# A hybrid block pair on one core: the recurrence's root from tanh(-x) and exp(2x), and gate tiles ahead of the first transposes in two attention layers

## The reference, cut to what matters

```
r = sigmoid(x W_a + b_a);  i = sigmoid(x W_x + b_x)
log_a = -8 * r * softplus(-lam)
a = exp(log_a);  u = sqrt(-expm1(2 * log_a)) * (i * x)
h[t] = a[t] * h[t-1] + u[t];   y = h * silu(x W_g)
```

```
S = scale * Q K^T + bias or mask;  P = softmax(S);  O = P V
y = (O * silu(h W_z)) W_out
```

## Time and profile before

| what | value |
|---|---|
| median of 3 runs | 2391.98 us |
| lowest, highest | 2387.72, 2394.45 us |
| the profiled execution | 2391.33 us |
| its span | 2389.6 us |
| mean granted TensorE clock | 0.944 |
| TensorE matmuls busy | 2102.4 us (88%) |
| VectorE busy | 1273.9 us (53%) |
| ScalarE busy | 889.1 us (37%) |
| GpSimd busy | 524.6 us (22%) |

### The profile page before, as it was taken

One profiled execution on the slowest core, in us unless ns is written; L12 is line 12 of the kernel. 1 busy time (PEld: TensorE's weight loads), 2 busy tenths in 40 slices (PEclk: granted clock), 3 DMA queues, 4 the chain that ended last, 5 costly groups with the idle time before them and its releaser, 6 DMA issues.

```text
span 2389.6 us, 25010 instructions
## 1 busy us (share of the span) xinstructions
PE 2102.4 (88%) x10118; PEld 1611.7 (67%) x10118; DVE 1273.9 (53%) x1756; ACT 889.1 (37%) x1281; POOL 524.6 (22%) x422
## 2 busy tenths in 40 slices
PE   5899998999988998999798886979879988878986
PEld 3687765788556887678597763767657755555865
DVE  6886664727389233544525446164455466544273
ACT  4225455311274223322322343256433344533232
POOL 3852121405146401232210101102021001102001
PEclk9999999999987998999899998989989999989998
DMA  2242110234221533535256421711212201122211
GB/s 110 87 156 78 36 54 18 91 108 152 90 88 53 159 106 106 176 115 163 92 146 172 98 79 44 160 36 53 71 58 87 90 18 36 36 71 97 88 71 53
DMA packets 53138, 215.26 MB, mean 90 GB/s; under 512 B 6048, under 2 KB 23104, under 8 KB 32672
## 3 DMA queue, kind: packets, MB, share of 16 engines
q1 hardware_dynamic: 22896, 162.54, 19.5%
q0 software_dynamic: 9488, 35.94, 5.4%
q10 hardware_dynamic: 20640, 15.19, 3.0%
HBM read 196.14 MB, written 17.50 MB: 89 GB/s over the span
## 4 chain that ended last, share of the span: by engine, by line
PE 59%; DVE 14%; ACT 4%; issue 3%; DMA 2%; ACTq 1%; POOL 1%; DVEq 0%; PEldq 0%
PE bank L477 16%; PE bank L478 16%; PE bank L479 16%; PE bank L476 2%; ACT ring_high L434 2%; DVE ring_low L439 2%; DVE root L1513 2%; DMA ring<-slabs 2%; DVE root L1204 1%; PE bank L1140 1%; PE bank L2761 1%; DVE sq L1208 1%; PE bank L2787 1%; ACTq L2085 1%; DVE lru_x L1526 1%
## 5 line engine op out<-in xcount | busy, mean ns | idle before, releaser
L439 DVE TENSOR_TENSOR ring_low<-ring,ring_high 128x2048 fp32r<-128x2048 f32 x136 | 329.8, 2426 | 473.2 <-ACT ring_high L434 473.2
L477 PE MATMUL bank<-h_high,ring_high 128*128 128x512 f32 x1248 | 512.7, 411 | 70.7 <-DVE ring_low L439 37.4
L434 ACT ACTIVATE ring_high<-ring 128x2048 fp32r<-128x2048 f32 x145 | 277.5, 1914 | 627.7 <-PE bank L479 582.5
L478 PE MATMUL bank<-h_low,ring_high 128*128 128x512 f32 x1248 | 497.4, 399 | 0.0
L479 PE MATMUL bank<-h_high,ring_low 128*128 128x512 f32 x1248 | 495.7, 397 | 0.0
L477 PEld LDWEIGHTS bank<-h_high,ring_high 128*128 128x128 f32 x1248 | 241.3, 193 | 155.1 <-issue 68.4
L478 PEld LDWEIGHTS bank<-h_low,ring_high 128*128 128x128 f32 x1248 | 242.3, 194 | 51.0 <-issue 3.5
L479 PEld LDWEIGHTS bank<-h_high,ring_low 128*128 128x128 f32 x1248 | 241.2, 193 | 52.5
L477 PE MATMUL bank<-gated_high,ring_high 128*128 128x512 f32 x256 | 106.1, 415 | 27.2 <-issue 20.8
L439 POOL TENSOR_TENSOR ring_low<-ring,ring_high 128x2048 fp32r<-128x2048 f32 x9 | 43.0, 4783 | 335.0 <-ACT ring_high L434 335.0
L478 PE MATMUL bank<-gated_low,ring_high 128*128 128x512 f32 x256 | 104.2, 407 | 0.0
(11 more groups left out here) (500 smaller groups left out, 4035.1 us busy)
## 6 DMA issues: line engine op xcount, KB each, us to landing
ring<-slabs SPq DMA_DIRECT2D x149, 1024.0 KB, 4.8
s_outputs<-s_ca POOLq DMA_DIRECT2D x4, 1152.0 KB, 8.1
x<-xT SPq DMA_DIRECT2D x2, 2048.0 KB, 9.1
s_b<-s_br POOLq DMA_DIRECT2D x8, 512.0 KB, 4.1
s_rows<-s_powers POOLq DMA_DIRECT2D x16, 256.0 KB, 6.9
s_inputs<-s_w POOLq DMA_DIRECT2D x8, 512.0 KB, 3.5
s_ck<-s_outputs POOLq DMA_DIRECT2D x1, 4096.0 KB, 23.5
s_wv<-s_inputs ACTq DMA_DIRECT2D x8, 512.0 KB, 6.0
```

The costliest lines, as they stand in the source:

```text
L434: act.activation(self.ring_high[:, self.splits_before[s] % AHEAD, :], self.ring[:, s % RING, :], ACT.Copy)\
L439: dve.tensor_tensor(self.ring_low[:, s % RING, :], self.ring[:, s % RING, :], self.ring_high[:, self.splits_before[s] % AHEAD, :].bitcast( ...
L477: pe.matmul(out, w[0], x[0], start=start, stop=False)
L478: pe.matmul(out, w[0], x[1], start=False, stop=False)
```

## The change

It does three things. In the recurrence q comes as (exp(2x) + 1) * tanh(-x), with the new exponential on ScalarE and one instruction on VectorE instead of three; ScalarE now writes q, so it waits for the scan of four tiles earlier. In the sliding-window stage z_0 and z_1 are computed after scores(1) and the loop computes z_(j+2) up to j = 5. In the latent stage z_0 comes after scores(1), and the loop computes z_(h/2+1) with scores(h+2), up to h = 12. Banks, weight order, evacuations and splits follow.

```diff
@@ more_sections
-    for j in range(9):
-        if j < 8:
-            cols = np.r_[256 * j + span(0, 64), 256 * j + 128 + span(0, 64)]
-            add("mla_kz", [("c_w_ukv", span(k * P), cols) for k in range(2)])
-        if j > 0:
-            add("mla_kz", tile("c_w_in", KD, span(1056 + (j - 1) * P)))
+    for j in range(8):
+        cols = np.r_[256 * j + span(0, 64), 256 * j + 128 + span(0, 64)]
+        add("mla_kz", [("c_w_ukv", span(k * P), cols) for k in range(2)])
+        add("mla_kz", tile("c_w_in", KD, span(1056 + j * P)))
@@ stage_lru, ratios (VectorE)
                     dve.wait_ge(th.sem, th.at(m))
-                    ln(dve, dve.tensor_scalar(q, t, 1.0, None, ALU.add))
-                    ln(dve, dve.reciprocal(q, q))
-                    dve.scalar_tensor_tensor(out=q, in0=t, scalar=2.0, in1=q, op0=ALU.mult, op1=ALU.mult)\
+                    dve.scalar_tensor_tensor(out=q, in0=q, scalar=1.0, in1=t, op0=ALU.add, op1=ALU.mult)\
                         .then_inc(rt.sem, 1)
@@ stage_lru, decays (ScalarE)
                     if m >= BUFS:
-                        act.wait_ge(rt.sem, rt.at(m - BUFS))
-                    C.achain.link(act, act.activation(t, L.R[:, m, :], ACT.Tanh, scale=-1.0))
+                        act.wait_ge(scanned.sem, scanned.at(m - BUFS))
+                    act.activation(t, L.R[:, m, :], ACT.Tanh, scale=-1.0)
+                    C.achain.link(act, act.activation(q, L.R[:, m, :], ACT.Exp, scale=2.0))
                     act.activation(L.R[:, m, :], L.R[:, m, :], ACT.Exp).then_inc(th.sem, 1)
@@ stage_swa, TensorE
             scores(0)
             scores(1)
+            for j in range(2):
+                C.gemm(pe, zb[j], C.H.tiles(KD), seen)
...
                 if j + 2 < NJ:
                     scores(j + 2)
-                C.gemm(pe, zb[j], C.H.tiles(KD), seen)
+                    C.gemm(pe, zb[j + 2], C.H.tiles(KD), seen)
@@ stage_swa, ScalarE
-            exps(0)
-            exps(1)
+            def evac_z(j):
+                C.split_high(act, zb[j][0])
+                C.full(act, zb[j][0])
+                act.activation(L.Z[:, j, :], C.bank[zb[j][0].b][:], ACT.Copy).then_inc(C.bank_read[zb[j][0].b], 1)
+
+            for j in range(2):
+                evac_z(j)
+                exps(j)
...
                     exps(j + 2)
+                    evac_z(j + 2)
@@ stage_mla, TensorE
             scores(0)
             scores(1)
+            C.gemm(pe, zb[0], C.H.tiles(KD), seen)
             C.read(pe, L.v_uses[-1])
...
                 if h + 2 < H:
                     scores(h + 2)
-                if h % 2 == 0:
-                    C.gemm(pe, zb[h // 2], C.H.tiles(KD), seen)
+                    if h % 2 == 0:
+                        C.gemm(pe, zb[h // 2 + 1], C.H.tiles(KD), seen)
@@ stage_mla, ScalarE (evac_z as above)
             keys(0)
             exps(0)
+            evac_z(0)
             exps(1)
...
                     exps(h + 2)
+                    if h % 2 == 0:
+                        evac_z(h // 2 + 1)
```

More of the change, by code:

```diff
@@ L1536, in decays @@
                 for m in range(b, b + NB):
-                    t = C.sq[:, m % BUFS, :]
+                    t, q = C.sq[:, m % BUFS, :], C.root[:, m % BUFS, :]
                     act.wait_ge(scaled.sem, scaled.at(m))
                     if m >= BUFS:
-                        act.wait_ge(rt.sem, rt.at(m - BUFS))
-                    C.achain.link(act, act.activation(t, L.R[:, m, :], ACT.Tanh, scale=-1.0))
+                        act.wait_ge(scanned.sem, scanned.at(m - BUFS))
+                    act.activation(t, L.R[:, m, :], ACT.Tanh, scale=-1.0)
+                    C.achain.link(act, act.activation(q, L.R[:, m, :], ACT.Exp, scale=2.0))
                     act.activation(L.R[:, m, :], L.R[:, m, :], ACT.Exp).then_inc(th.sem, 1)
@@ L2545, in stage_swa @@
     NJ = 8
-    sb, pb, ob, zb = [[C.take_bank() for _ in range(TC)] for _ in range(2)], [], [], []
+    sb, pb, ob, zb = [[C.take_bank() for _ in range(TC)] for _ in range(2)], [], [], [C.take_tile(KD) for _ in range(2)]
     for j in range(NJ):
@@ L2550, in stage_swa @@
             sb.append([C.take_bank() for _ in range(TC)])
-        zb.append(C.take_tile(KD))
+            zb.append(C.take_tile(KD))
         ob.append(C.take_bank())
@@ L2683, in _ @@
                     exps(j + 2)
-                C.split_high(act, zb[j][0])
-                C.full(act, zb[j][0])
-                act.activation(L.Z[:, j, :], C.bank[zb[j][0].b][:], ACT.Copy).then_inc(C.bank_read[zb[j][0].b], 1)
+                    evac_z(j + 2)
             C.full(act, ob[NJ - 1])
@@ L2843, in _ @@
             C.lows_before(pool, [u for u, _ in kb + zb])
[L2844 to L2847, removed]
+            for k, z in zip(kb, zb):
+                C.split_low(pool, k[0])
                 C.split_low(pool, z[0])
@@ L2872, in exps, with evac_z @@
                 ins.then_inc(ex.sem, 1)
+            def evac_z(i):
+                u = zb[i][0]
+                C.split_high(act, u)
+                C.full(act, u)
+                act.activation(L.Z[:, i, :], C.bank[u.b][:], ACT.Copy).then_inc(C.bank_read[u.b], 1)
             keys(0)
             exps(0)
+            evac_z(0)
             exps(1)
```

## The result

The changed kernel takes 2351.32 us (median of 4 runs, 2348.43 to 2356.01) where the kernel before, run beside it, takes 2390.25 (median of 4). The ratio is 0.983, with a 95% interval of 0.9808 to 0.9853. The prediction was 2356 with a range of 2345 to 2368.

A forecast was written before the change was run, and what follows sets the result against it. VectorE was taken to set the recurrence's pace, with TensorE waiting for low parts. From 2391.33, 34 less (recurrence), 2 less (sliding window) and no change (latent) gave 2355.3, stated as 2356, range 2345 to 2368.

The forecast's parts named there:

- The start: Recurrence: first slab's rounding ends at 683.9, its low part at 687.0, before TensorE needs it; the 8.7 us wait goes.
- The pace: Recurrence: VectorE, slowed by GpSimd most of the interval, gives a low part every 12.0 us; ScalarE needs 11.4.
- The new wait for the scan: Recurrence: ScalarE's wait for the scan four tiles earlier costs nothing; the rival of engines taking turns, 2403, had 0.02.
- The lock rival: Recurrence: VectorE and GpSimd exclude each other, pace 13.9, clock falls, 23.5 us less, 2366 in all; chance 0.18.
- The third exponentials: Sliding-window stage: they start at 1589.8, 2.7 us late, because the first two wait for gate tiles' copies.
- And so do all others: Sliding-window stage: all later exponentials stay 2.7 us late, 12.06 us apart per head pair, up to 1650.2.
- The tail: Sliding-window stage's end: from last exponentials at 1650.2, remaining work ends at 1665.8 where 1669.30 stood, 3.5 us less.
- up to 5: Sliding-window stage's end: last transposes and products, after a wait of some 4 us, take up to 5 us more at low clock.
- The low part that held VectorE at the end: Sliding-window stage: it held VectorE 1.6 us at the end; coming earlier, it makes 3.5 us less into 5.1 less.
- the warm clock: Latent stage: the first transposes stay at 1915.3 but run with a warm clock, 0.6 us less.
- copies and split: Latent stage's last heads: waiting for copies costs 1.8 us; the last split, now at head 12, costs 2.3 to 5.
- The rival that the gate tiles pay in full: Both attentions: TensorE ends the stages, 8 us less in window, 5 in latent, recurrence 36, 2342 in all; chance 0.12.

The follow-up runs named there:

- the two experiments: The changed kernel without the new second exponential on ScalarE, 2350.67 us, and the changed kernel without GpSimd's product with silu(g), 2350.75 us; one run each.
- The experiment with the late split: The changed kernel with the latent stage's split after z_7 asked for at head 14 instead of 12: 2345.57 us, single run.
- all orders: The changed kernel with window exponentials before copies, last latent split at head 14, and k_3's split behind the key copies: 2339.14 us, ratio 0.9781.

## Why the prediction was right

**The recurrence** was predicted at 34 us less and gave 33.0. The start held: the rounding was to end at 683.9, that is to begin at 682; it began at 684.20, which is 682.1 when the 2.1 us of the late first tanh are taken off. The wait of 8.7 us is gone. The pace was to be 12.0, with VectorE under GpSimd as its cause; it is 12.03, and the two experiments show that cause. That the number is so close is in part luck. The working had 10.4 us from product to low part and two multiplies at their undisturbed 0.69, 11.8, and 12.0 was a choice near it. In the changed kernel product to low part takes 717.14 to 725.85, 8.7 us, and the multiplies 713.74 to 717.14, 3.4 us: 1.7 less and 2.0 more, two errors that cancel. ScalarE was to need 11.4 and needs 11.48. TensorE was to wait some 2.7 us in all and waits 2.6, with the clock at 1.00. The eighth slab was to start at 745.9 and starts at 749.22, 747.1 with the shift taken off: 1.2 late. The first of these low parts ran from 686.74 to 689.4 (687.3 shifted back, 687.0 predicted), the second came 12.43 later and the next three 12.02 each, which puts the seventh slab's at 735.8 instead of 735.0; the last 0.4 lie in that slab.

**The new wait for the scan** costs nothing: ScalarE shows no wait at all between 690 and 735 us in the changed kernel. That it is real is seen only without the second exponential, where ScalarE stands 0.93 us for it.

**The lock rival** (13.9 a pair) was wrong, but half of it is there. Undisturbed, as the shortest rows of each line have it, VectorE's work for a pair is 2.29 + 2 x (1.22 + 0.66 + 0.69) = 7.4 us and GpSimd's 2 x (1.29 + 0.61 + 1.29) = 6.4 (the 0.61 is from before). One behind the other that is 13.8; the pair takes 12.03. The Trainium skill (SBUF — State Buffer, SBUF: two separate sides) tells of an exclusive lock for whole instructions. The two multiplies at 3.48 and the gain of 0.54 when GpSimd's product goes agree with it. That 12.03 is 1.8 below 13.8 shows that these durations do not exclude each other in full. Some of the 1.8 is the ends of operations, which overlap on one engine too (711.19 + 2.63 = 713.82, and the next starts at 713.74); how much is left for operations that run side by side is not shown.

**The sliding-window stage** was predicted at 2 less, between 5 less and 1 more, and gave 4.0 (3.6 alone). The sum lands in its range by errors that cancel, so here the terms matter:
- z_0's copy ahead of the table load, and the load ahead of the exponentials: as predicted. The first transposes start 1549.98 - 1529.90 = 20.1 us after the first scores, 18.4 before (1576.72 - 1558.3): 1.7 late, 1.5 predicted, and the wait 3.3 where 3 was said.
- The third exponentials come 32.4 us after the first scores, 28.8 before (1587.14 - 1558.3): 3.6 late instead of 2.7. The first row of VectorE above has the reason: a step that takes 0.17 us elsewhere takes 1.04 while GpSimd makes a low part (1549.12 to 1554.32). I had not asked where the first split's low part would fall.
- "And so do all others" was the step that failed. The fourth exponentials lose another 13.56 - 12.06 = 1.5 us: VectorE waits 1.14 + 0.17 for TensorE's scores, because behind the wait of 3.3 the transposes and scores ran at the low clock (scores 4.80, 2.55 at full clock). From there it is 12.06 four times in a row, (1624.12 - 1575.84) / 4 = 12.07. So the chain was 5.1 late, not 2.7.
- The tail from the last exponentials to the table load takes 14.3, where 15.6 was predicted, although its first product ran at the low clock (3.16 instead of 1.80). I had added evacuations that in part run beside TensorE. At this end TensorE waits once, 2.57 us, where 3 to 5 was said. Of the "up to 5" allowed for a low clock in this tail 1.4 came; the late scores at the front of the chain, 1.5, stood in no term.
- The low part that held VectorE at the end is gone, 1.6 less, as predicted.

By terms: -5.1 predicted for a clean stage, 0.9 for the low part on VectorE, 1.5 for the late scores, 1.4 for the slow product, and 2.7 less for the tail give -4.0.

**The latent stage** was predicted at no change, -2 to +1, and gave 2.1 less. The first transposes stand where they stood: 1882.83 - 1871.70 = 11.13 us after the first scores, 11.12 before. The wait fell by 5.5 (6.54 to 1.07), predicted 5.45. TensorE's busy time in the stage fell by 0.6 (153.96 to 153.37), and 0.6 was predicted, but this agreement is luck: the 0.6 stood for the warm clock at the first transposes, and from these to the next scores TensorE is busy 2.68 us instead of 4.36, 1.7 less, at a granted clock of 1.00 instead of 0.65. Before (first row; columns as in the earlier trace rows) and after:
```profile
1915.28:1920.32 5.04, 4.36 (x16) 3.60 (x16) 2.21 (x7) 1.59 (x4) 0.00 (x0) 0.65 0.01 3
...
1882.82:1886.18 3.36, 2.68 (x16) 2.08 (x16) 2.21 (x7) 3.11 (x10) 0.00 (x0) 1.00 0.00 0
```
The slow product at the last heads (3.71 instead of 2.34) takes 1.4 of it back. The new wait there is 3.9, where copies and split were put at 1.8 + 2.3 to 5. The experiment with the late split parts the two: 1.7 for the copies, and for the split 2.2 of wait and 1.4 of clock, 3.6. By terms: -1.7 for the warm clock, -5.5 for the tile, 1.7 for the copies, 3.6 for the split and -0.3 for the rest of TensorE's busy time give -2.2 (2.1 less measured). So the term that was too small is the warm clock, 0.6 instead of 1.7. The waits for keys come to 16.5 us before and after. Four low parts fell on VectorE's multiplies at 3.5 us (at 1898.21, 1964.53, 2008.10 and 2030.14), not five as predicted: the second missed them.

**The rival that the gate tiles pay in full** (8 less in the window stage, 5 in the latent stage) did not come true, with 4.0 and 2.1. But the two stages gave that much once the orders were changed: 114.6 - 104.6 = 10.0 and 180.3 - 174.4 = 5.9 us.

**The sum** came out 4.7 us above the median. The latent stage gave 2.1 more and the window stage 2.0 more than I said, the recurrence 1.0 less; 0.7 was rounding up, and the sum starts from a run 1.1 us slower than this batch's median.

## What to carry to other kernels

Where an engine sets the pace, count what its neighbour on the same memory does to it: the pace here was neither VectorE's own work (7.4 us) nor the sum with GpSimd's (13.8), but 12.03, and rows of operations under the same neighbour gave it in advance to 0.3 us (11.8), though by two errors of 1.7 and 2.0 that cancel. When work is put into a gap, look at what it stands in front of on the engine that copies the result out of PSUM, and at where the splits move: putting two ScalarE calls in the other order and asking for one split two heads later took another 9.8 us from the two stages, where the gate tiles had taken 6.1. A reordered stage must be read to its last wait, since part of the gain was given back there, at the last heads of the latent stage for one: by a new wait and by the low clock behind it.

## What the runs showed of the hardware

The same wait does not always bring the low clock. Behind a wait of 3.17 us for keys, scores of the same form took 2.43 us (before, at 2029.51), 3.57 (before, at 1985.97), 3.80 (after) and 4.64 (all orders). Behind 2.75 us they took 3.87 before and 2.43 after. Nor is it chance alone: with one order of the latent stage's keys and scores the same waits brought it in seven of eight profiles (the first of 3.2 us was followed by scores of 4.63 or 4.64, the 2.75 by 2.42 or 2.43, the next 3.17 by 3.75 to 3.90, the last 3.17 by 2.42 or 2.43), and in the eighth, the kernel with the window's exponentials first, the first was followed by 2.42 and the last by 3.91. What decides is not shown. It moves an unchanged stage by some us: the sliding-window stage with the same code took 107.5, 103.3 and 104.6 us in three kernels, and the product behind its last wait of 2.5 us took 3.28, 2.01 and 2.01.

In the recurrence of the changed kernel a scan takes 1.22 to 2.35 us, longer while GpSimd works, and GpSimd's subtraction takes 1.29 to 3.22 us while VectorE works. A table load costs 1.28 us, and the next activation starts 0.01 us after it (672.21 + 1.28 = 673.49, next at 673.50). A tanh behind a sigmoid (671.02, then 671.59) or a silu (686.00, then 686.48) has no load in front, the exponential behind it has (672.21, 687.11), and between the exponentials and tanh of one pair there is none.
